# Memory's product ahead of x's tiles: reordering the first block of a two-layer kernel

## The chip, the cores and the metric

The kernel runs on one core of a Trainium2 chip. The metric is the device time of one execution in microseconds (us). Three runs of the kernel before gave 2940.59, 2943.91 and 2949.29; the median is 2943.91.

## The reference

Two residual layers on `x` of 1024 positions by 1024 channels, in float32. The first layer mixes an RWKV-7 branch and a short convolution, adds a cross attention over 256 memory vectors and an MLP; the second layer has a gated delta rule and a stick-breaking attention. The change touches only how the first things that the first layer needs come about. Cut to these:

```
h = rms_norm(x, norm_mix)              # x: 1024 x 1024
p = h @ w_in                           # its first three column tiles used here: lora inputs
mem_n = rms_norm(mem, norm_mem)        # mem: 256 x 1024
k, v = split(mem_n @ w_kv, 2)          # w_kv: 1024 x 2048
```

and `rms_norm(x, g) = x * rsqrt(mean(x * x) + 1e-6) * g`.

## The kernel before

The program is a row of blocks with a barrier of all engines between them. The first block is built by `start_to_loras`. It has three helpers: `Start` loads and turns `mem` and `x`, `MemoryKeys` makes the product of `mem` with `w_kv`, and `MixNorm` makes the normalised x, `h`.

Every product is made of float32 numbers as three products of rounded numbers (type fp32r): a number is split into a rounded part (`hi`) and a remainder (`lo`), and TensorE adds hi by hi, lo by hi and hi by lo. ScalarE makes the rounded part and VectorE subtracts it from the number for the remainder.

The work of the block, in the order of the kernel before:

- **Loads.** SyncE's queue issues the ten tiles of 128 rows (two of `mem`, eight of `x`, 512 KB each), then the first two rows of weights of `w_kv`, then some of the small vectors (gains and biases), then further rows. There are 16 rows of weights: 0 to 7 for the keys, 8 to 15 for the values, each of 128 by 1024. They go through four raw buffers, and row j from 4 on waits until row j - 4 has been split (`fetch`). ScalarE's queue issues the other 18 loads of small vectors. All vectors lie as rows of one tile, `vec_rows`, which TensorE turns once (`vec`).
- **Turning.** TensorE transposes each of the ten tiles in eight pieces into a pair of PSUM banks (`turn`, L4299), and VectorE copies the pair out (`copy`, L4338). ScalarE sums the squares of each tile (`square`, L4319). After eight tiles TensorE turns the vectors (L4311) and then tiles 8 and 9.
- **Memory.** ScalarE multiplies `mem` by its gain and rounds (`mem_hi`, L4330), and VectorE makes `mem_lo` (L4352). The gain comes from the turned vectors. Only when all eight parts are done and all ten tiles copied does the first product begin.
- **Rows.** Per row of `w_kv`: ScalarE rounds (`kv_hi`, L4394), VectorE subtracts (`kv_lo`, L4398), TensorE does 12 matmuls of 128x512 (`products`, L4408). The pairs hi and lo have three buffers, so ScalarE begins row j when TensorE has finished row j - 3.
- **Between rows.** Behind row 1 TensorE spreads the 1024 factors of x's norm over all partitions (`spread_row`, L4466), from a diagonal that VectorE makes (`factors`, L4457), and ScalarE keeps them (`keep_row`, L4472). For each of eight parts k of x, VectorE scales (`scale`, L4480), ScalarE rounds (`round`, L4485) and VectorE subtracts (`subtract`, L4490). In rows 4 to 15 VectorE does one of these two operations per row, in turn; parts 6 and 7 come behind row 15. Behind row 9 TensorE turns the keys (`turn_keys`, L4425); ScalarE has taken them from the banks (L4417) and copies them back (L4432), and SyncE stores them, behind the fetch of row 12 and ahead of those of rows 13 to 15.
- **w_in.** Three tiles of `w_in` go through `round_tile` on ScalarE and `subtract_tile` on VectorE (L177), and TensorE makes 48 matmuls with each (L280). VectorE mixes their results for the lora stage (L4648, L4650), and GpSimd splits the next block's first two tiles (L161, L164).

GpSimd makes constants and masks in the first 14 us (L2205 and its neighbours).

Of the kernel before, what the change touches and what calls it, by code (L numbers as in the profile page):

```python
# [11 lines left out]
P = 128  # L12
SEQ = 1024
HALF = 512
D = 1024
# [17 lines left out]
    ("r_k", 4), ("ln_x_w", 4), ("ln_x_b", 4), ("conv_w", 12), ("norm_xattn", 8), ("norm_mem", 8),  # L33
# [4151 lines left out]
class Vectors:  # L4185
# [40 lines left out]
    def load(self, eng, group):  # L4226
        eng.wait_ge(self.cleared, 1)
        for dst, src in self.pieces(group):
            eng.dma_start(dst, src).then_inc(self.loaded[group], 16)


class Start:
# [4 lines left out]
    def __init__(self, c):  # L4237
        self.c, d = c, c.dram
        self.tiles = [d["mem"][0, t * P:(t + 1) * P, :] for t in range(2)] + [d["x"][0, t * P:(t + 1) * P, :] for t in range(TILES)]
        self.xin = at(c, 24576, "x_in", [P, len(self.tiles), D])  # L4240
# [8 lines left out]
        self.vec_turned, self.vec_copied = c.sem("vec_turned"), c.sem("vec_copied")  # L4249
        self.mem_rounded, self.mem_split = c.sem("mem_rounded"), c.sem("mem_split")  # L4250
# [4 lines left out]
    def load(self, sp):  # L4255
        for t, src in enumerate(self.tiles):
            sp.dma_start(self.xin[:, t], src).then_inc(self.x_in[t], 16)
# [35 lines left out]

    def turn(self, pe, t):
        c = self.c
        pe.wait_ge(self.x_in[t], 16)
        wait(pe, self.copied, t - 1)
        for k in range(KT):
            last = pe.transpose(c.ps[:, 2 * (t % 2) + k // 4, (k % 4) * P:(k % 4 + 1) * P], self.xin[:, t, k * P:(k + 1) * P],  # L4299
                                c.ident[:])  # L4300
        last.then_inc(self.turned, 1)

    def pe(self, pe):
        c = self.c
        pe.wait_ge(c.begun, 1)
        for t in range(8):
            self.turn(pe, t)
        for g in range(2):
            pe.wait_ge(self.vectors.loaded[g], self.vectors.total[g])
        for s in range(2):  # L4310
            last = pe.transpose(c.ps[:, 4, s * P:(s + 1) * P], self.vectors.rows[:, s, :], c.ident[:])  # L4311
        last.then_inc(self.vec_turned, 1)
        for t in range(8, 10):
            self.turn(pe, t)

    def square(self, act, t):
        act.wait_ge(self.x_in[t], 16)
        wait(act, self.squared, t - 1)
        act.activation(self.junk[t % 2][:], self.xin[:, t], ACT.Square, accum_out=self.sums[:, t:t + 1]).then_inc(self.squared, 1)  # L4319

    def act(self, act):
        c = self.c
        for t in range(8):
            self.square(act, t)
        act.wait_ge(self.vec_turned, 1)
        act.copy(c.vec[:], c.ps[:, 4, 0:2 * P]).then_inc(self.vec_copied, 1)
        act.wait_ge(self.vec_copied, 1)
        act.wait_ge(self.copied, 2)
        for k in range(KT):
            act.activation(self.mem_hi[:, k], self.mem_t[:, k], ACT.Copy, scale=vec(c, "norm_mem", k)).then_inc(self.mem_rounded, 1)  # L4330
        for t in range(8, 10):
            self.square(act, t)

    def copy(self, dve, t):
        c = self.c
        dve.wait_ge(self.turned, t + 1)
        dst = c.x[:, :, (t - 2) * P:(t - 1) * P] if t > 1 else self.mem_t[:, :, t * P:(t + 1) * P]
        dve.tensor_copy(dst, c.ps[:, 2 * (t % 2):2 * (t % 2) + 2, :].rearrange("p b (k n) -> p (b k) n", n=P)).then_inc(self.copied, 1)  # L4338

    def dve(self, dve):  # L4340
        c = self.c
        for t in range(8):
            self.copy(dve, t)

        dve.wait_ge(self.copied, 2)
        for k in range(KT):
            if k == 3:
                self.copy(dve, 8)
            if k == 6:
                self.copy(dve, 9)  # L4350
            dve.wait_ge(self.mem_rounded, k + 1)
            dve.scalar_tensor_tensor(out=self.mem_lo[:, k], in0=self.mem_t[:, k], scalar=vec(c, "norm_mem", k),  # L4352
# [3 lines left out]
class MemoryKeys:  # L4356
# [6 lines left out]
    def __init__(self, c, start):  # L4363
# [5 lines left out]
        self.keys = at_h(c, 32768 + 20480, "mem_keys", [P, KT, N_MEM])  # L4369
# [2072 lines left out]
```

## Time and profile before

| what | us |
|---|---|
| median of three runs (2940.59 to 2949.29) | 2943.91 |
| the profiled execution | 2940.22 |
| its span, first to last instruction | 2938.5 |
| TensorE busy in the span (96%) | 2808.3 |
| VectorE busy | 1604.6 |
| ScalarE busy | 1120.5 |
| GpSimd busy | 1325.8 |
| the first block, from the start to the next block's first matmul | 114.75 |

The profile is of one execution. Busy times are summed over the instructions of an engine. A row of the timeline gives the start, the time from the first instruction's start to the last one's end of a group that belongs together, the engine (PE is TensorE, PEld its weight loads, DVE VectorE, ACT ScalarE, POOL GpSimd, SPq SyncE's queue), line and operation, and in brackets how long the engine was idle before and what ended it. The granted clock is that of TensorE as a share of 2.4 GHz.

### The profile page before, as it was taken

How to read it: one execution, taken by the hardware profiler on the slowest of the kernel's cores; microseconds unless marked ns; L12 is line 12 of the kernel's file. 1: busy time of each engine (PE TensorE's matmuls, PEld its weight loads, DVE VectorE, ACT ScalarE, POOL GpSimd, SP SyncE). 2: the span in 40 equal slices, each digit the busy share in tenths (PEclk: the TensorE clock that was granted, in tenths of full speed). 3: DMA queues.
4: the chain of work that ended last, by engine and by line, in shares of the span. 5: the costliest groups of instructions: out<-in, count | busy, mean ns of one | idle time of the engine just before them, and what ended most of it. 6: DMA issues, size and time to landing. Idle time of an engine off the chain costs nothing. (4 is left out here: it accounts for less than half of the span.)

```text
span 2938.5 us, 48523 instructions
## 1 busy us (share of the span) xinstructions
PE 2808.3 (96%) x19890; PEld 2247.0 (76%) x19890; DVE 1604.6 (55%) x1907; ACT 1120.5 (38%) x1781; POOL 1325.8 (45%) x987
## 2 busy tenths in 40 slices
PE   7999788999999999999999999999999899999999
PEld 6777677778878876788888888677787678866677
DVE  5555444863465434555555554767768435357661
ACT  5433223554311123424444444333323335567310
POOL 1331213677645430347777775211211457745552
PEclk9999999999999999999999999999999999999999
DMA  5342433343171111122322233131234524421243
GB/s 206 108 158 95 129 89 95 109 139 90 36 229 43 50 51 44 43 79 88 99 88 92 88 97 104 36 94 52 86 99 139 164 85 123 127 83 62 68 139 127
DMA packets 318509, 288.93 MB, mean 98 GB/s; under 512 B 47858, under 2 KB 270249, under 8 KB 315610
## 3 DMA queue, kind: packets, MB, share of 16 engines
q1 hardware_dynamic: 318042, 285.89, 31.8%
q8 instruction: 153, 2.51, 0.4%
q14 instruction: 58, 0.48, 0.1%
q10 hardware_dynamic: 256, 0.07, 0.0%
HBM read 214.86 MB, written 70.65 MB: 97 GB/s over the span
## 5 line engine op out<-in xcount | busy, mean ns | idle before, releaser
L855 POOL TENSOR_TENSOR op_lo<-w_raw,op_hi 128x512 fp32r<-128x512 f32 x172 | 222.1, 1299 | 238.3 <-ACT op_hi L844 237.7
L280 PE MATMUL ps<-h_hi,w_hi 128*128 128x512 f32 x960 | 310.3, 404 | 5.3 <-POOL w_lo L177 3.7
L280 PE MATMUL ps<-h_lo,w_hi 128*128 128x512 f32 x960 | 297.9, 392 | 0.0
L280 PE MATMUL ps<-h_hi,w_lo 128*128 128x512 f32 x960 | 297.5, 391 | 0.0
L161 POOL TENSOR_TENSOR w_hi<-w_raw,ones 128x1024 fp32r<-128x1024 f32 x54 | 132.0, 2444 | 300.9 <-PE ps L280 161.2
L280 PEld LDWEIGHTS ps<-h_hi,w_hi 128*128 128x128 f32 x960 | 179.2, 189 | 62.2 <-issue 22.9
L280 PEld LDWEIGHTS ps<-h_hi,w_lo 128*128 128x128 f32 x960 | 181.2, 189 | 38.9
L280 PEld LDWEIGHTS ps<-h_lo,w_hi 128*128 128x128 f32 x960 | 181.0, 189 | 38.7
L177 POOL TENSOR_TENSOR w_lo<-w_raw,w_hi 128x1024 fp32r<-128x1024 f32 x30 | 73.1, 2437 | 303.8 <-ACT w_hi L172 303.8
L164 POOL TENSOR_TENSOR w_lo<-w_raw,w_hi 128x1024 fp32r<-128x1024 f32 x54 | 145.4, 2693 | 4.2
L1784 DVE TENSOR_TENSOR x_t<-x_t,ps 128x512 f32<-128x512 f32 x144 | 96.2, 685 | 83.7 <-PE ps L910 56.8
L844 ACT CAST op_hi<-w_raw 128x512 fp32r<-128x512 f32 x167 | 102.5, 620 | 84.6 <-POOL w_raw L860 27.6
L280 PE MATMUL ps<-branch_hi,w_hi 128*128 128x512 f32 x384 | 120.2, 394 | 7.0 <-POOL w_lo L164 5.5
L5370 DVE RECIPROCAL p_root<-p_root 128x1024 f32<-128x1024 f32 x16 | 104.8, 6547 | 36.3 <-ACT p_root L5224 36.1
L860 POOL TENSOR_TENSOR w_raw<-w_raw 128x512 f32<-128x512 f32 x92 | 122.3, 1329 | 3.6
L280 PE MATMUL ps<-branch_lo,w_hi 128*128 128x512 f32 x384 | 118.7, 391 | 0.0
L280 PE MATMUL ps<-branch_hi,w_lo 128*128 128x512 f32 x384 | 118.7, 390 | 0.0
L6198 POOL TENSOR_TENSOR sb_weight<-sb_weight,sb_left 128x512 f32<-128x512 f32 (+3 forms) x96 | 84.9, 896 | 71.2 <-DVE sb_left L6352 70.6
L6352 DVE TENSOR_TENSOR_SCAN sb_left<-ps,sb_left,ones 128x512 f32<-128x512 f32 (+3 forms) x96 | 92.4, 1004 | 34.2 <-ACT ps L6298 32.8
L897 PE MATMUL ps<-h_hi,op_hi 128*128 128x512 f32 x256 | 99.8, 390 | 0.0
L897 PE MATMUL ps<-h_hi,op_lo 128*128 128x512 f32 x256 | 99.6, 389 | 0.0
L897 PE MATMUL ps<-h_lo,op_hi 128*128 128x512 f32 x256 | 99.6, 389 | 0.0
(736 smaller groups left out, 7321.1 us busy)
## 6 DMA issues: line engine op xcount, KB each, us to landing
w_raw<-in_w_in_dram SPq DMA_DIRECT2D x91, 512.0 KB, 4.8
mix_gates<-mix_sig SPq DMA_DIRECT2D x64, 256.0 KB, 2.3
w_raw<-in_w_up_dram SPq DMA_DIRECT2D x32, 512.0 KB, 4.2
w_raw<-in_w_down_dram SPq DMA_DIRECT2D x32, 512.0 KB, 3.5
kv_raw<-in_w_kv_dram SPq DMA_DIRECT2D x16, 512.0 KB, 6.0
mix_gate_b<-mix_gates SPq DMA_DIRECT2D x32, 256.0 KB, 4.6
mlp_t3h<-mlp_kept_t SPq DMA_DIRECT2D x6, 1024.0 KB, 5.0
mlp_t3l<-mlp_kept_t SPq DMA_DIRECT2D x6, 1024.0 KB, 4.9
```

The lines of the kernel that those rows point to most:

```text
L161: pool.tensor_tensor(c.w_hi[:, s], c.w_raw[:, s], c.ones[:].unsqueeze(1).broadcast_to([P, KT, P]), ALU.mult).then_inc(c.w_rounded, 1)
L164: pool.tensor_tensor(c.w_lo[:, s], c.w_raw[:, s], c.w_hi[:, s].bitcast(F32), ALU.subtract).then_inc(c.w_split, 1)
L177: eng.tensor_tensor(c.w_lo[:, s], c.w_raw[:, s], c.w_hi[:, s].bitcast(F32), ALU.subtract).then_inc(c.w_split, 1)
L280: last = pe.matmul(o, w[:, s, k], a[:, k - offset, (half + h) * width:(half + h + 1) * width], start=(k == kts[0] and w is c.w_hi and a is ...
L844: act.copy(self.hi(o)[:], src).then_inc(self.rounded, 1)
L855: pool.tensor_tensor(self.lo(o)[:], src, self.hi(o)[:].bitcast(F32), ALU.subtract).then_inc(self.pooled, 1)
L860: pool.tensor_tensor(out, a, b, op).then_inc(self.pooled, 1)
L897: last = pe.matmul(out, w[:, k], a(k), start=start and k == 0 and w is w_hi and a is hi, stop=stop and k == HK - 1 and w is w_lo, skip_gro ...
L1784: dve.tensor_tensor(part, part, ps[:, down_banks[g, d][bank][side]], ALU.add).then_inc(down_free, 1)
L5370: v.mark(dve.reciprocal(root[:], root[:]))
L6198: pool.tensor_tensor(weight[:, n % 4, hd, 0:width], weight[:, n % 4, hd, 0:width], left[:, n % 2, hd, 1:width + 1], ALU.mult).then_inc(wei ...
L6352: dve.tensor_tensor_scan(l[:, hd, 0:width][:, ::-1], ps[:, 2 * (n % 2) + hd, 0:width][:, ::-1], c.ones[:, 0:1].broadcast_to([P, width]), l ...
```

## The change

The vector `norm_mem` gets a load and a transpose of its own, so `mem` no longer waits for all vectors. SyncE issues the two tiles of `mem`, then rows 0 and 1 of `w_kv`, and then x's tiles with rows 2 and 3 among them. Six of the first group's vector loads move from ScalarE's queue to SyncE's, and SyncE's vector loads stand behind row 4. TensorE turns only `mem` ahead of row 0; x's tiles are turned behind rows 0 to 5, and the vectors and the spreading stand behind row 6. Each row of the keys waits only for its own part of `mem`. ScalarE's and VectorE's queues are put in a matching order, so that the sums of squares stand between the roundings of rows 3 to 7. The scaling of x begins at row 8 and takes a part per row: at rows 9 to 15 VectorE does kv_lo, one scaling and one remainder. The remainders of the three `w_in` tiles go to GpSimd. The keys, the x tiles and the gain have other places in memory, and the store of the keys now stands ahead of row 15 only. The core of the diff:

```
-        self.xin = at(c, 24576, "x_in", [P, len(self.tiles), D])
+        self.xin = [at_h(c, 12288 + 4096 * t, f"x_in{t}", [P, D]) if t < 4 else
+                    c.nc.alloc_sbuf_tensor_at(f"x_in{t}", [P, D], F32, offset=c.w_base + 4096 * (t - 4)) for t in range(len(self.tiles))]
...
+    def banks(self, t):
+        return 2 * t if t < 2 else 4 + 2 * (t % 2)
+
     def turn(self, pe, t):
+        c, bank = self.c, self.banks(t)
+        pe.wait_ge(self.x_in[t], 16)
+        if t == 3:
+            pe.wait_ge(self.gain_copied, 1)
+        if t > 3:
+            pe.wait_ge(self.copied, t - 1)
...
+    def turn_gain(self, pe):
         c = self.c
+        pe.wait_ge(self.gain_loaded, 16)
+        pe.transpose(c.ps[:, 6, 0:KT], self.gain_rows[:], c.ident[0:KT, 0:KT]).then_inc(self.gain_turned, 1)
+
+    def turn_vectors(self, pe):
...
+        pe.wait_ge(self.copied, 10)
...
+    def take_gain(self, act):
+        act.wait_ge(self.gain_turned, 1)
+        act.copy(self.gain[:], self.c.ps[:, 6, 0:KT]).then_inc(self.gain_copied, 1)
+        act.wait_ge(self.gain_copied, 1)
+        act.wait_ge(self.copied, 2)
...
     def fetch(self, sp, j):
-        if j < 2:
-            pass
-        elif j < self.RAW:
-            sp.wait_ge(self.start.turned, 2)
-            sp.wait_ge(self.start.squared, 2)
-        else:
+        if j >= self.RAW:
             sp.wait_ge(self.split, j - self.RAW + 1)
...
     def products(self, pe, j):
         pe.wait_ge(self.split, j + 1)
+        if half == 0:
+            pe.wait_ge(self.start.mem_split, k + 1)
...
             @block.sync
-                start.load(sp)
-                for j in range(2):
-                    memory.fetch(sp, j)
+                start.load(sp, 0, 1)
+                memory.fetch(sp, 0)
+                memory.fetch(sp, 1)
+                start.load(sp, 2, 3)
+                memory.fetch(sp, 2)
+                start.load(sp, 4, 5)
+                memory.fetch(sp, 3)
+                start.load(sp, 6, 7, 8, 9)
+                memory.fetch(sp, 4)
                 start.vectors.load(sp, 1)
-                for j in range(2, 4):
-                    memory.fetch(sp, j)
+                start.vectors.load(sp, 0, 12)
+                memory.fetch(sp, 5)
                 start.store_masks(sp)
-                for j in range(4, 13):
+                for j in range(6, 15):
                     memory.fetch(sp, j)
                 sp.wait_ge(memory.keys_copied, 4)
                 sp.dma_start(c.scratch["mem_k"] ...
-                for j in range(13, 16):
-                    memory.fetch(sp, j)
+                memory.fetch(sp, 15)
...
             @block.gpsimd
                 start.pool(pool)
+                weights.subtract_tile(pool, 0, 0)
+                pool.wait_ge(memory.keys_stored, 16)
+                for u in range(1, 3):
+                    weights.subtract_tile(pool, 0, u)
...
             @block.tensor
-                start.pe(pe)
-                pe.wait_ge(start.mem_split, KT)
-                pe.wait_ge(start.copied, 10)
+                pe.wait_ge(c.begun, 1)
+                start.turn(pe, 0)
+                start.turn(pe, 1)
+                start.turn_gain(pe)
                 for j in range(16):
                     memory.products(pe, j)
-                    if j == 1:
+                    for t in ((2,), (3,), (4,), (5, 6), (7,), (8, 9))[j] if j < 6 else ():
+                        start.turn(pe, t)
+                    if j == 6:
+                        start.turn_vectors(pe)
                         norm.spread_row(pe)
...
             @block.scalar
-                start.vectors.load(act, 0)
-                start.act(act)
+                start.load_gain(act)
+                start.vectors.load(act, 0, 0, 12)
                 memory.round(act, 0)
+                start.take_gain(act)
+                start.round(act, 0, 1)
                 memory.round(act, 1)
+                start.round(act, 2, 3, 4, 5, 6, 7)
+                memory.round(act, 2)
+                for j in range(3, 8):
+                    for t in range(2 * (j - 3), 2 * (j - 2)):
+                        start.square(act, t)
+                    memory.round(act, j)
                 norm.root(act)
+                memory.round(act, 8)
+                start.take_vectors(act)
                 norm.keep_row(act)
-                for j in range(4, 16):
+                for j in range(9, 16):
                     memory.round(act, j)
-                    if j == 10:
+                    if j == 9:
...
-                    if j % 2:
-                        norm.round(act, (j - 5) // 2)
+                    norm.round(act, j - 9)
...
             @block.vector
-                start.dve(dve)
+                start.copy(dve, 0)
+                start.copy(dve, 1)
                 memory.subtract(dve, 0)
+                start.subtract(dve, 0, 1)
                 memory.subtract(dve, 1)
+                start.subtract(dve, 2, 3, 4, 5, 6, 7)
+                start.copy(dve, 2)
+                memory.subtract(dve, 2)
+                start.copy(dve, 3)
+                for j in range(3, 8):
+                    memory.subtract(dve, j)
+                    for t in ((4,), (5, 6), (7,), (8, 9), ())[j - 3]:
+                        start.copy(dve, t)
                 norm.factors(dve)
-                memory.subtract(dve, 2)
-                memory.subtract(dve, 3)
-                for j in range(4, 16):
+                for j in range(8, 16):
                     memory.subtract(dve, j)
-                    if j % 2 == 0:
-                        norm.scale(dve, (j - 4) // 2)
-                    else:
-                        norm.subtract(dve, (j - 5) // 2)
-                    if j == 13:
-                        dve.wait_ge(memory.keys_stored, 16)
-                weights.subtract_tile(dve, 0, 0)
-                for k in range(6, 8):
-                    norm.scale(dve, k)
-                    norm.subtract(dve, k)
-                for u in range(1, 3):
-                    weights.subtract_tile(dve, 0, u)
+                    norm.scale(dve, j - 8)
+                    if j > 8:
+                        norm.subtract(dve, j - 9)
+                norm.subtract(dve, 7)
```

## Rows read from the trace of the kernel before

**Rows 1.** The page's costliest groups; the last number before the bar is the mean ns.

```profile
L177 POOL TENSOR_TENSOR w_lo<-w_raw,w_hi 128x1024 fp32r<-128x1024 f32 x30 | 73.1, 2437 | 303.8 <-ACT w_hi L172 303.8
```

**Rows 2.** Busy time by windows of the first block; start:end, length, engines, clock, DMA, GB/s.

```profile
29.70:34.50 4.80, 4.78 (x12) 3.87 (x13) 3.60 (x4) 2.10 (x3) 0.00 (x0) 0.56 0.68 211
34.50:81.60 47.10, 44.69 (x201) 36.17 (x200) 31.95 (x27) 25.66 (x30) 0.00 (x0) 1.00 0.53 168
81.60:114.70 33.10, 32.83 (x145) 26.84 (x143) 18.34 (x9) 14.02 (x15) 11.42 (x5) 1.00 0.33 98
10.00:20.00 10.00, 5.27 (x41) 4.20 (x39) 7.08 (x6) 7.96 (x16) 3.80 (x16) 1.00 1.03 397
```

**Rows 3.** Timeline of TensorE up to its first product.

```profile
4.71 6.30 PE L4299 MATMUL ps<-ident,x_in 128*128 128x128 f32 x32 [4.71 <-DMA x_in<-in_mem_dram]
11.47 2.20 PE L4299 MATMUL ps<-ident,x_in 128*128 128x128 f32 x16 [0.47 <-DVE x_t L4338]
...
20.90 0.66 PE L4311 MATMUL ps<-ident,vec_rows 128*128 128x128 f32 x2 [4.75 <-DMA vec_rows<-in_sb_k_gain_dram]
...
29.72 1.19 PE L4408 MATMUL ps<-kv_hi,mem_hi 128*128 128x512 f32 x2 [5.29 <-DVE kv_lo L4398]
```

**Rows 4.** Timeline of TensorE from its first product to the next block.

```profile
37.28 1.88 PE L4466 MATMUL ps<-mix_diag,ones 128*128 128x512 f32 x4
38.60 1.03 PE L4408 MATMUL ps<-kv_hi,mem_hi 128*128 128x512 f32 x2
...
60.82 1.91 PE L4425 MATMUL ps<-ident,w_raw 128*128 128x128 f32 x16
62.48 0.71 PE L4408 MATMUL ps<-kv_hi,mem_hi 128*128 128x512 f32 x2
...
73.31 0.73 PE L4408 MATMUL ps<-kv_hi,mem_hi 128*128 128x512 f32 x2 [2.41 <-DVE kv_lo L4398]
...
81.62 0.62 PE L280 MATMUL ps<-h_hi,w_hi 128*128 128x512 f32 x2
...
114.75 0.70 PE L280 MATMUL ps<-h_hi,w_hi 128*128 128x512 f32 x2 [0.32 <-PEq L4521]
```

**Rows 5.** Timeline of VectorE, ScalarE and SyncE's queue, 8 to 98 us.

```profile
8.40 1.22 DVE L4338 COPY mem_t<-ps 128x1024 f32<-128x1024 f32 x1 [0.48 <-PE ps L4299]
...
27.27 0.87 DVE L4352 SCALAR_TENSOR_TENSOR mem_lo<-mem_t,vec,mem_hi 128x256 fp32r<-128x256 f32 x2
...
31.17 1.23 DVE L4457 TENSOR_TENSOR mix_diag<-ident,square_sums 128x1024 f32<-128x1024 f32 x1
...
39.20 1.01 ACT L4472 COPY mix_row<-ps 128x1024 f32<-128x1024 f32 x1 [3.37 <-PE ps L4466]
...
56.58 2.42 ACT L4417 ACTIVATE w_raw<-ps,square_sums 128x512 f32<-128x512 f32 x4
...
64.51 3.03 SPq L4388 DMA_DIRECT2D kv_raw<-in_w_kv_dram  x3
...
74.31 1.22 DVE L4398 TENSOR_TENSOR kv_lo<-kv_raw,kv_hi 128x1024 fp32r<-128x1024 f32 x1
75.44 1.28 DVE L4480 SCALAR_TENSOR_TENSOR mix_whole<-x_t,vec,mix_row 128x1024 f32<-128x1024 f32 x1
76.64 1.22 DVE L4398 TENSOR_TENSOR kv_lo<-kv_raw,kv_hi 128x1024 fp32r<-128x1024 f32 x1
...
97.12 3.30 DVE L4650 SCALAR_TENSOR_TENSOR lora_mixed<-lora_mixed,vec,lora_plain 128x1024 f32<-128x1024 f32 x1
```

**Rows 6.** Timeline of GpSimd: two steps of the masks, and a remainder.

```profile
10.78 0.58 POOL L2205 TENSOR_SCALAR_AFFINE_SELECT level_temp<-level_temp 128x64 f32<-128x64 f32 x2
...
96.09 3.25 POOL L164 TENSOR_TENSOR w_lo<-w_raw,w_hi 128x1024 fp32r<-128x1024 f32 x1
```

**Rows 7.** Loads issued at 0.8 and at 64.5 us; the last number is us to landing.

```profile
x_in<-in_mem_dram SPq DMA_DIRECT2D x1, 512.0 KB, 3.8
...
kv_raw<-in_w_kv_dram SPq DMA_DIRECT2D x1, 512.0 KB, 6.4
```

More of the change, by code:

```diff
@@ L4224, in pieces, with load @@
                     done += m
-    def load(self, eng, group):
+    def load(self, eng, group, first=0, last=None):
         eng.wait_ge(self.cleared, 1)
-        for dst, src in self.pieces(group):
+        for dst, src in list(self.pieces(group))[first:last]:
             eng.dma_start(dst, src).then_inc(self.loaded[group], 16)
@@ L4253, in __init__, with load, load_gain @@
         scratch(c, "masks", [P, N_MASKS, BLOCK])
[L4255 to L4257 removed]
+    def load(self, sp, *which):
+        for t in which:
+            sp.dma_start(self.xin[t][:], self.tiles[t]).then_inc(self.x_in[t], 16)
+    def load_gain(self, act):
+        act.dma_start(self.gain_rows[:], self.c.dram["norm_mem"].rearrange("a (n p) -> (a n) p", p=P)).then_inc(self.gain_loaded, 16)
     def store_masks(self, sp):
@@ L4318, in square @@
         wait(act, self.squared, t - 1)
[L4319 to L4324, printed above, removed]
-        act.wait_ge(self.vec_turned, 1)
[L4326 to L4332, printed above, removed]
+        act.activation(self.junk[t % 2][:], self.xin[t][:], ACT.Square, accum_out=self.sums[:, t:t + 1]).then_inc(self.squared, 1)
@@ new lines, in take_gain, with take_vectors, round @@
+    def take_gain(self, act):
[3 more added lines that the diff above has]
+        act.wait_ge(self.copied, 2)
+    def take_vectors(self, act):
+        act.wait_ge(self.vec_turned, 1)
+        act.copy(self.c.vec[:], self.c.ps[:, 6, 0:2 * P]).then_inc(self.vec_copied, 1)
+    def round(self, act, *which):
+        for k in which:
+            act.activation(self.mem_hi[:, k], self.mem_t[:, k], ACT.Copy, scale=self.gain[:, k:k + 1]).then_inc(self.mem_rounded, 1)
@@ L4334, in copy @@
     def copy(self, dve, t):
-        c = self.c
+        c, bank = self.c, self.banks(t)
         dve.wait_ge(self.turned, t + 1)
         dst = c.x[:, :, (t - 2) * P:(t - 1) * P] if t > 1 else self.mem_t[:, :, t * P:(t + 1) * P]
[L4338 to L4350, printed above, removed]
+        dve.tensor_copy(dst, c.ps[:, bank:bank + 2, :].rearrange("p b (k n) -> p (b k) n", n=P)).then_inc(self.copied, 1)
@@ L4351, in dve, with subtract @@
+    def subtract(self, dve, *which):
+        for k in which:
             dve.wait_ge(self.mem_rounded, k + 1)
-            dve.scalar_tensor_tensor(out=self.mem_lo[:, k], in0=self.mem_t[:, k], scalar=vec(c, "norm_mem", k),
+            dve.scalar_tensor_tensor(out=self.mem_lo[:, k], in0=self.mem_t[:, k], scalar=self.gain[:, k:k + 1],
                                      in1=self.mem_hi[:, k].bitcast(F32), op0=ALU.mult, op1=ALU.subtract).then_inc(self.mem_split, 1)
```

46 lines of the change are left out of this document (20 added, 26 removed).

## The prediction

> **What bounds the kernel now.** The windows come first [rows 2], behind one line of the page that the second part needs [rows 1]. The kernel is one span of 2938.5 us in which TensorE is nearly always busy, and the change touches only its first 114.75 us, the block that `start_to_loras` builds. A barrier ends that block: the next block's first matmul starts at 114.75, 0.32 us after TensorE's last one here [rows 4]. VectorE and ScalarE are busy for 18.3 and 14.0 us of the last 33.1 [rows 2]. So the block ends when TensorE ends, and a microsecond taken out of TensorE's queue comes off the whole time, because later blocks are not touched and their first loads are issued by events that move with it.
>
> The timeline of TensorE's own instructions shows where it isn't working [rows 3, 4]. Up to its first product with the memory at 29.72 it waits 4.71 us for the first tile, 0.47 and once more less for VectorE to empty banks, 4.75 for the small vector loads that landed behind twelve big ones, and 5.29 for VectorE, which rounds all of `mem` before the first weights. From 29.72 on it stands still once, 2.41 us before row 13. The 51.90 us from 29.72 to 81.62 are: row 0 in 4.80 us (12 matmuls at a granted clock of 0.56, so mostly at 1.2 GHz) [rows 2]; spreading the mix factors 1.32 (37.28 to 38.60); turning the keys 1.66 (60.82 to 62.48); the stall of 2.41; what is left, 41.7, is 15 rows of 2.78. After 81.62 come 33.1 us of w_in products with no gap.
>
> **The change, part by part.** TensorE's work is the same but for one tiny transpose; what moves is the order. The eight x tiles are turned between rows 0 to 5 instead of ahead of row 0. The sum is when the chain of products ends, counted forward.
>
> *First product.* The memory tiles are still loads one and two. The first tile landed 3.8 us after its issue, and 512 KB at the 397 GB/s of a full queue is 1.3 us [rows 2, 7]. Counting tiles in the new order, w row 0 lands at about 7.3 and row 1 at 8.6; all of x is in by 22, row 4 by 23.3, and behind it twelve small vector loads. In the trace before seven of those and the two last big tiles lay between x and the vectors' 20.90, which leaves about 0.2 us each, so row 5 lands near 27. TensorE reaches rows 4 and 5 only after 27 and 31. The transfers are cover, not bound. VectorE's second copy of `mem` still runs 8.40 to 9.62 [rows 5]. Behind it come kv_lo 0 (1.22) and the first mem_lo (0.45, two took 0.87), so the first product could start at 11.3. ScalarE is in time: it issues 12 vector loads instead of 18 and is ready at about 7.3.
>
> There is one thing on that path that the rows only show elsewhere. At 97.12 an operation of VectorE with two SBUF inputs took 3.30 us where its like takes 1.28, and GpSimd's at 96.09 took 3.25 against a mean of 2.44 [rows 1, 5, 6]. VectorE's ended 1.1 us after GpSimd's, as if each had the memory to itself. In the early block GpSimd is making masks until about 14.4, in steps of about 0.3 us [rows 6], and VectorE's subtractions now fall into that time (before, only copies from PSUM did). Each of the two on the path can wait 0 to 0.35 us. Taken: 0.3 together, 11.6; bounds 11.3 and 12.1. The later six mem_lo and kv_lo 1 slip by at most the 4 us of masks that are left, to 18; row 2 needs its weights at 21.4. The Trainium skill's page "SBUF — State Buffer", section "SBUF: two separate sides", says that the pair of ports is an exclusive lock, taken by a VectorE operation with two SBUF inputs against a GpSimd one that reads SBUF. By it the selects count and the memsets don't, and the start would be 11.6; if it didn't hold for selects, 11.3. No row of the trace before has a subtraction against a select.
>
> *Rows 0 to 6.* Row 0 costs 4.80 again: TensorE's first 32 transposes took 6.30 us where later ones take 1.10 for eight [rows 3], so it starts slow, and it stops at 8.3, before that had lifted, and waits over 3 us. If the clock were up, row 0 would cost 2.78. From 11.6: row 0 to 16.4, six rows of 2.78 to 33.1, eight tiles of 1.10 to 41.9. VectorE keeps up in it: of its 1.22 us per copy and per kv_lo, two in a 3.9 us turn, never more than three.
>
> *The factors.* Tiles 8 and 9 are turned before row 6, that is by 39.1. VectorE then has copy 8, copy 9 and kv_lo 7 in its queue (38.1 to 41.7), then the reciprocal 0.22 and the diagonal 1.23, to 43.2. TensorE turns the vectors (0.45) to 42.3 and waits 1.0 for it: 43.3. Spreading costs 1.32, row 7 ends at 47.4. Before, this wait did not exist; its cost is what is late behind the last copies.
>
> *Rows 8 to 15.* Here is the place to look. Before, VectorE did three operations for every two TensorE rows. Now rows 9 to 15 each bring three: kv_lo, a scaling, a remainder. From one start to the next these take 1.13 to 1.14, 1.20 and 1.14 [rows 5], 3.48 us a row against TensorE's 2.78. VectorE's lead: the row copy (1.01 us, begun 1.9 after the spreading starts) [rows 5] ends at 46.2, and scaling 0 starts there. Kv_lo 9 and scaling 1 follow to 49.8. Remainder 0 waits for ScalarE, which must first take row 8's four banks (2.42 us from 47.5) [rows 5] and round 0, to 50.9. From there a row every 3.48: kv_lo 10, 11, 12, 13, 14, 15 are ready at 53.3, 56.8, 60.2, 63.7, 67.2, 70.7. TensorE would be ready for them at 54.5 (after turning the keys), 57.3, 60.1, 63.0 and so on: it waits 0.1 for row 12 and 0.7 each for rows 13, 14, 15. Total 2.2.
>
> *The old stall.* Row 13 waited 2.41 us because its load stood on SyncE's queue behind the store of the keys: issued at 64.5, it landed at 70.9 [rows 5, 7]. Now only row 15 and the w_in tiles are behind that store, which is issued near 58.7; row 15 lands by 65 and w_in 0 at 67 to 70.5 against a need at 69.4. So 2.41 goes away.
>
> *w_in's first tile.* Its remainder goes to GpSimd, 2.44 us a tile instead of 1.22 [rows 1]. Rounded at about 70.4, it is ready at 73.1, or at 74.3 if one operation of VectorE goes first. TensorE is there at 73.5. Taken 0.3, bounds 0 and 1. Tiles 1 and 2 have 10 us each to spare, and the next block's tiles, queued on GpSimd behind them, are split long before their use.
>
> Sum: 11.6 + 4.8 + 41.7 (15 rows) + 8.8 + 0.45 + 1.0 + 1.32 + 1.66 + 2.2 + 0.3 = 73.8, against 81.62. The gain is 7.8 us. In other words: the first product comes 18.1 us sooner and a stall of 2.4 goes, 9.25 us of transposes fall into the chain instead, and 3.5 us of new waits are made. The profiled execution's own 2940.22 becomes 2932.4; it lies 3.7 us under the median of the runs, so of 2943.91 it leaves 2936.1.
>
> **The rivals.** 0.3%, here 8.8 us, is about what a measurement of this kernel tells from no change, and the forecast lies just inside it.
>
> (a) *The clock is up sooner.* Row 0 then costs 2.78, and 2.0 more is gained: 9.8, 2934.1. For it: only 3.3 us lie between the last transpose and the first product. Against: a pause of 4.75 us before was followed by slow transposes and one of 5.3 by a slow row [rows 2, 3], and the engine has not been fast yet. With the chance that some wait (factors, row 12 on) is smaller than reckoned: 0.36 for over 8.8 us. The Trainium skill's "TensorE: Matmul & The Clock Gate", section "What's actually happening", has the slow clock as the default that activity lifts; by that, the row stays slow.
>
> (b) *VectorE paces more than I count.* Handshakes with ScalarE of 0.3 us on each of the 21 operations of rows 9 to 15 would make a row 4.4 us: 6 us gone of which TensorE's slack takes none, and the gain is about 2, 2942. Before, such handshakes showed as short idle times of VectorE, but when it had time to spare. Chance 0.13.
>
> (c) *The change does not do what it says:* weights land behind x and TensorE stands. A start at 20 instead of 11.6 would eat it, at 2943 or so. Full-queue speed speaks against it; w row 0 would have to land 8 us late. Chance 0.03.
>
> (d) *Slower.* Mixing transposes and fp32r products with waits in between could keep TensorE at 1.2 GHz through rows 1 to 6 and all x tiles. Each row then costs 2.0 more and eight tiles 0.8 each: 18 us, net 10 slower, 2954. It decides from the point where more than four rows stay slow (8 us: nothing gained). Against: TensorE has no wait between 11.6 and 42.3, and in the trace before the clock rose 4 us into such a stretch. With all else that could go so: 0.04.
>
> **How the numbers follow.** The forecast, 5 to 8.8 us gained, has 0.44; (a) 0.36; (b) 0.13; (c) 0.03; (d) 0.04. Likeliest time 2936, its own range 2933.5 to 2940 with the uncertainty of the start (0.8), of the clock (2), of the tile (1) and of the waits. The range for 8 in 10 takes in (a) and (b): 2930.5 to 2942.5. Faster by over 0.3%: 0.37; within: 0.58 (forecast, b, c and the smaller half of measuring spread); slower: 0.05.
>
> **What the profile would show.** First product at 11.3 to 12.1 with kv_lo 0 or mem_lo as its releaser. Row 0 in 4.8 us, the clock at 1.0 from about 16. A wait of 1.0 ahead of the spreading, released by the diagonal. No stall at row 13 by a load, but short waits on kv_lo in rows 12 to 15. First w_in matmul at 73.8, next block at 106.9. Wrong would be: rows 1 to 6 at 5 us (d), VectorE idle between its operations after 47 (b), a wait of TensorE released by a load (c), subtractions of 2 us and more before 15 us (the shared memory port, larger than taken).

## The result, and the profile after

The changed kernel takes 2928.36 us (median of 5 runs, 2924.89 to 2929.46) against 2943.91 (2940.59 to 2949.29, 5 runs): a ratio of 0.9946, interval 0.9935 to 0.9956, 15.6 us less. The forecast was 2936.1 with a range down to 2930.5, so the time lies 2.1 us below the range, on the side of "faster" that had 0.37. The profiled execution takes 2927.02, its span 2925.3; TensorE is busy 2803.3 us of it.

The first block of the changed kernel, TensorE's timeline. It answers to [rows 3, 4]; x and a number at a line's end tell how many instructions are drawn together.

```profile
4.63 3.65 PE L4312 MATMUL ps<-ident,x_in 128*128 128x128 f32 x16 [4.63 <-DMA x_in<-in_mem_dram]
8.21 0.27 PE L4318 MATMUL ps<-ident,mem_gain_rows 8*128 8x8 f32 x1
11.22 1.19 PE L4410 MATMUL ps<-kv_hi,mem_hi 128*128 128x512 f32 x2 [2.73 <-DVE mem_lo L4357]
...
16.41 1.04 PE L4312 MATMUL ps<-ident,x_in 128*128 128x128 f32 x8
17.21 0.70 PE L4410 MATMUL ps<-kv_hi,mem_hi 128*128 128x512 f32 x2
...
27.30 1.91 PE L4312 MATMUL ps<-ident,x_in 128*128 128x128 f32 x16
28.96 0.71 PE L4410 MATMUL ps<-kv_hi,mem_hi 128*128 128x512 f32 x2
...
39.92 0.38 PE L4326 MATMUL ps<-ident,vec_rows 128*128 128x128 f32 x2
41.48 1.95 PE L4472 MATMUL ps<-mix_diag,ones 128*128 128x512 f32 x4 [1.18 <-issue]
42.87 1.02 PE L4410 MATMUL ps<-kv_hi,mem_hi 128*128 128x512 f32 x2
...
59.03 0.73 PE L4410 MATMUL ps<-kv_hi,mem_hi 128*128 128x512 f32 x2 [0.17 <-DVE kv_lo L4398]
...
62.50 0.73 PE L4410 MATMUL ps<-kv_hi,mem_hi 128*128 128x512 f32 x2 [0.45 <-DVE kv_lo L4398]
...
72.29 0.62 PE L280 MATMUL ps<-h_hi,w_hi 128*128 128x512 f32 x2
```

The first product starts at 11.22 instead of 29.72, released by VectorE's `mem_lo`. From there TensorE has one wait of 1.18 ahead of the spreading and four short ones on `kv_lo`, and it comes to w_in at 72.29, 9.3 us sooner than in [rows 4]. The waits of TensorE up to 110 us (total, times, longest) say that nothing else is left:

```profile
PE ps L4312 <- DMA x_in<-in_mem_dram: 4.6, 1, 4.6
PE ps L4410 <- DVE mem_lo L4357: 2.7, 1, 2.7
PE ps L4410 <- DVE kv_lo L4398: 1.5, 4, 0.4
PE ps L4472 <- issue: 1.2, 1, 1.2
PE ps L280 <- PEq L4528: 0.3, 1, 0.3
```

The next block starts at 105.41. So 9.3 us come from the first block by these two profiles, and 15.6 by the medians. The rest of the text is about the difference.

### The profile page after: what moved, and what is told of

It is laid out like the page before. It is cut to its first block and busy times, and to the rows that moved or that the text cites. A ratio compares the mean times of both kernels' runs of the same rounds, so it can differ in the third digit from the quotient of the medians.

```text
span 2925.3 us, 48530 instructions
## 1 busy us (share of the span) xinstructions
PE 2803.3 (96%) x19891; PEld 2241.3 (77%) x19891; DVE 1595.4 (55%) x1904; ACT 1119.1 (38%) x1782; POOL 1335.0 (46%) x990
## 5 line engine op out<-in xcount | busy, mean ns | idle before, releaser
L177 POOL TENSOR_TENSOR w_lo<-w_raw,w_hi 128x1024 fp32r<-128x1024 f32 x33 | 80.3, 2434 | 361.7 <-ACT w_hi L172 361.7
L164 POOL TENSOR_TENSOR w_lo<-w_raw,w_hi 128x1024 fp32r<-128x1024 f32 x54 | 144.3, 2672 | 4.2
```

The source lines that it names most:

```text
L164: pool.tensor_tensor(c.w_lo[:, s], c.w_raw[:, s], c.w_hi[:, s].bitcast(F32), ALU.subtract).then_inc(c.w_split, 1)
```

## The experiments

**The spread of both kernels, and the block's end moved.** The first question was whether the 15.6 us are real and whether they hang on when the later blocks start. Four kernels: both kernels again, and both with ScalarE copies behind the block's work, so that the block ends later. In the changed one:

```
                weights.done(act, 0, 2)
                for n in range(14):
                    c.a_steps.wait(act)
                    c.a_steps.mark(act.copy(c.ps[:, 7, 0:512], c.x[:, 0, 0:512]))
```

(in the kernel before 2 copies of 320.)

> The changed kernel once more, unaltered. In its first profile the next block began 9.4 us sooner than before, but the span was 13.2 us shorter and the median of the runs 15.5 us. Theory L (luck): the 4 to 6 us beyond the first block come from TensorE's slow-clock stretches, which fall differently on the later blocks in each execution; then this ratio is nearer 0.9968 (9.4 us) and this profile's later part differs from the first one's by some microseconds. Theory S (systematic): the later blocks are really shorter in the changed kernel, and the ratio is 0.9946 again. First block either way: next block's first matmul at 105.4, within 0.2.

> The changed kernel with 14 copies of 128x512 one after another on ScalarE at the end of its first block, behind TensorE's last product there (they compute nothing that is used): some 9.4 us of pause, so that the later blocks start when they do in the kernel before. Theory L: time equals that of the kernel before, ratio 1.000, later part of the profile 2820 to 2824 us like any other. Theory S by start time (the later blocks' slow-clock stretches depend on when they start): ratio 1.000 too, but e4 then gains about 5 us. Theory S by code (something in the changed program makes later blocks shorter wherever they start): ratio 0.998, 6 us under before.

> The kernel before, unaltered, for a second profile and five more runs. Both theories: ratio 1.000. What it is to show is the spread of the part behind the first block: theory L expects that part (2823.7 us in the first profile) to differ by 2 to 4 us here, with the slow-clock stretches in other places; theory S expects 2823 to 2829 again and the same places.

> The kernel before with two copies of 128x320 on ScalarE at the end of its first block: about 1 us of pause. [...] Theories L and S by code: ratio 1.000 to 1.0005, 1 us slower.

Measured: the changed kernel 2927.25 (2922.8 to 2936.39, 6 runs; ratio 0.996, 0.9945 to 0.9976); the padded one 2935.83 (12 runs, 0.999, 0.998 to 1.0); the kernel before 2941.92 (11 runs) and with its pad 2943.95 (12 runs), against 2939.89 in 29 runs on that chip. The pad of about 8.6 us (next block at 114.03) costs 8.6 us by the medians, 8.8 by the means, no more. So the gain is real, some 12 to 16 us by the pairs of medians, and in this pair the time follows the block's end one for one (the last kernel below does not bear that out). The small pad costs 2.0, against some 1 us of it: not to be told apart. A third set of runs of the changed kernel was taken later:

> The changed kernel once more beside e10, to set its ratio firmer and for a third profile. Theory L (9.4 to 11.5 us in the first block, where the kernel before has one or two more slow-clock stretches; later blocks the same on average): ratio 0.9961 to 0.9968. Theory S: 0.9946.

It took 2924.14 (2920.84 to 2930.08, 5 runs), ratio 0.9948 (0.9934 to 0.9962). Over the three chips on which the changed kernel ran, 54 runs of the kernel before have a mean of 2941.3 (standard deviation 3.4) and 16 of the changed one 2927.5 (4.0): 13.8 with a standard error of 1.1.

The second profile of the kernel before has the same start as the first and a longer stall. It spreads the factors at 37.02 (37.28 in [rows 4]), and row 13 begins at 73.05 behind a pause of 2.39, but then four pairs in it run at half clock, 0.85 us apart, which the first profile does not have behind its 2.41:

```profile
37.02 1.88 PE L4466 MATMUL ps<-mix_diag,ones 128*128 128x512 f32 x4
...
73.05 0.73 PE L4408 MATMUL ps<-kv_hi,mem_hi 128*128 128x512 f32 x2 [2.39 <-DVE kv_lo L4398]
...
74.54 1.03 PE L4408 MATMUL ps<-kv_hi,mem_hi 128*128 128x512 f32 x2
75.38 1.05 PE L4408 MATMUL ps<-kv_hi,mem_lo 128*128 128x512 f32 x2
...
77.94 0.64 PE L4408 MATMUL ps<-kv_hi,mem_lo 128*128 128x512 f32 x2
...
116.09 0.70 PE L280 MATMUL ps<-h_hi,w_hi 128*128 128x512 f32 x2 [0.32 <-PEq L4521]
```

Four unpadded profiles of the kernel before (two of them of shortened kernels, below) have the next block at 114.75, 116.09, 116.05 and 116.58, mean 115.9; five of the changed kernel at 105.41, 104.62, 105.58, 104.35 and 104.66, mean 104.9. The block is 11.0 us shorter on average, not 9.3. Of the 1.1 that the kernel before needs beyond its first profile, 0.4 arise before the spreading (37.02 to 38.43, mean 37.7) and 0.7 at the old stall: the slow pairs above in one, a pause of 3.03 and 3.07 instead of 2.41 in the two others. The changed kernel's other 0.5 is row 0, which took 4.34 to 4.42 in three of its five profiles instead of 5.19.

**Where the rest is: kernels that end early.** The later blocks are left out: `build` ends behind the first block (cut1) or behind the scan (cut2) and writes `c.x` out.

```
-        late = first_block(c)
-        renew(c)
-        second_block(c, out, late)
+        cut_block(c)
+        write_out(c, out)
```

> The kernel before, ended behind its first block: all later blocks are left out, and x is written out as it lies. Its time is for the difference to e13. Theory L (all that is systematic is in the first block): the difference of the medians is 13 to 14 us. Rival (the first block gives what the profiles show and the rest lies further on or is chance): 9.3 to 11.5.

> The changed kernel, ended behind its first block in the same way. Theory L: 13 to 14 us under e12. Rival: 9.3 to 11.5 us under it. About 125 us in all.

> The kernel before, ended behind the scan (three blocks: start, features, scan; the rest is left out). About 520 us. For the difference to e15: if the scan's slow-clock stretches favour the changed kernel's start time, 13 to 15 us; if the scan only adds chance, the same difference as e12 and e13, with a spread of 2 to 4 us from run to run.

> The changed kernel, ended behind the scan in the same way. 9 to 12 us under e14 if the scan adds chance alone, 13 to 15 if it favours the earlier start.

Cut behind the first block: 129.81 (129.51 to 131.32) against 119.40 (118.66 to 120.39), 10.4 us (11.0 by the means). Behind the scan: 520.07 (517.51 to 524.56) against 504.68 (504.49 to 507.39), 15.4 us. About 5 us are thus gained in features and scan, by a change that does not touch them. One candidate was the moment at which they start. So the changed kernel was started late: 16 copies of ScalarE go ahead of its first load, SyncE waits for them, the first tile is turned at 15.78, the next block begins at 117.33.

```
+                act.wait_ge(filled, 1)
+                for n in range(16):
+                    wait(act, late, n)
+                    act.copy(c.ps[:, 7], c.x[:, 0, 0:HALF]).then_inc(late, 1)
...
+                sp.wait_ge(late, 16)
```

> e15's kernel (the changed one, ended behind the scan) with 16 copies of 128x512 one after another on ScalarE ahead of its first load, for which all loads wait: everything starts 10 to 11 us later, about where the scan of the kernel before starts. If the scan's length follows from when it starts: 520 us, like e14. If it follows from the program: 504.7 + 10.5 = 515, with a spread under 2 us. If it is chance: 515 to 520 with a spread of 2 to 3.

> e14 again (the kernel before, ended behind the scan). Chance: a median anywhere from 516 to 522. Otherwise 520 again.

> e15 again (the changed kernel, ended behind the scan). Chance: a median anywhere from 504.5 to 510, and a difference to e17 nearer 10.4 than 15.4. Otherwise 504.7 again, and 15 us under e17.

The late one took 516.92 (515.82 to 519.29); the two others, again, 522.96 (517.99 to 524.76) and 505.2 (503.29 to 509.89). All runs of the pair cut behind the scan together, 10 and 10, have means of 521.4 and 505.6: 15.8 us, 4.8 more than the 11.0 behind the first block, with a standard error of 1.1. The next block of the late kernel starts 12.4 us after the 104.9 of the others, and 505.6 + 12.4 = 518.0: it is late by its delay and keeps the short scan, although its scan begins later than in the kernel before (next block at 117.33 against 115.9). At this one later moment, at least, the start is not the cause.

The profiles say in part what differs in the scan, and not why. The features take 185.4 us in every profile but that of the padded changed kernel, where they take 2.2 more. The scan took 204.6, 199.9, 207.4, 200.9 and 204.3 in profiles of the kernel before (the third is the padded one) and 201.3, 207.7, 200.7, 199.8, 198.3, 200.4 (padded) and, in the late one, 200.6 of the changed kernel. In each there are stretches at half clock, near the scan's start and at other places from one execution to the next. The longest scans are of both kinds, and seven profiles against five don't separate them; the cut runs do, by 4.8 us.

It is not the clock that separates them. Both kernels cut behind the scan, from the scan's first matmul to its last and in one step of it (before, then changed; the figures behind the length are the five engines, TensorE first, and the clock behind them):

```profile
301.72:500.26 198.54, 161.03 (x5665) 141.90 (x5665) 84.25 (x192) 57.89 (x120) 49.07 (x57) 0.97 0.35 91
419.82:433.33 13.51, 10.78 (x394) 9.80 (x398) 4.99 (x11) 3.85 (x8) 2.85 (x4) 1.00 0.43 115
```

```profile
290.02:487.46 197.44, 162.59 (x5665) 143.62 (x5665) 84.33 (x192) 57.89 (x120) 48.80 (x57) 0.96 0.35 92
410.13:421.34 11.21, 10.51 (x394) 9.66 (x398) 4.86 (x11) 3.85 (x8) 2.84 (x4) 1.00 0.51 139
```

TensorE's busy time is not less in the changed kernel (162.5 to 167.7 us in its seven profiles, 161.0 to 165.1 in the five of before); it stands idle less, 33.2 to 37.6 us, mean 34.9, against 36.0 to 40.0, mean 37.7. One place differs beyond chance, the step from the eighth to the ninth copy of `scan_y`: 13.4 to 14.5 us in all five, 11.0 to 12.3 in all seven. The step ahead of it is shorter in the kernel before (10.6 to 11.0 against 11.0 to 12.1), so the two together give 1.5 us. The waits of TensorE in the step (before, then changed):

```profile
PE ps L2573 <- issue: 1.3, 1, 1.3
PE ps L2618 <- issue: 1.0, 1, 1.0
PE ps L2573 <- DVE scan_ab L2821: 0.5, 1, 0.5
```

```profile
PE ps L2573 <- issue: 0.4, 1, 0.4
PE ps L2573 <- DVE scan_ab L2821: 0.3, 1, 0.3
```

"Issue" is a wait for nothing that the profile shows: 2.2 to 2.7 us in the step before, 0.2 to 1.4 after. What it is stays open.

**The order alone.** All x tiles turned and copied ahead of row 0; gain, loads and everything else as in the change.

```
                 start.turn_gain(pe)
+                for t in range(2, 10):
+                    start.turn(pe, t)
                 for j in range(16):
                     memory.products(pe, j)
-                    for t in ((2,), (3,), (4,), (5, 6), (7,), (8, 9))[j] if j < 6 else ():
-                        start.turn(pe, t)
```

(VectorE: the copies 2 to 9 go ahead of `memory.subtract(dve, 2)`.) This kernel and the next three ran once each. Single runs of one kernel have a standard deviation of 3 to 5 us, so the argument goes by the start of the next block in the profile, which moves by 1.2 us in the changed kernel.

> The changed kernel with one part undone: x's eight tiles are turned and copied ahead of row 0 again (the early gain, the order of the loads and all the rest stay). Theory A (the gain is the time in which the tiles' turning and landing lie beside rows): the last tile lands at 22, the first product comes at about 23 to 24 instead of 11.2, and the rows lose eight tiles of 0.8 each, so w_in begins 5 to 6 us later than 72.3, at about 78, and the next block at 111. A second stretch of slow clock would add 2. Rival: the rows are held by VectorE and ScalarE anyway and most of the gain stays: next block at 106 to 107.

One run, 2935.49 (before on that chip 2941.93); the next block starts at 108.12, 2.7 later than with the change. TensorE:

```profile
11.75 3.68 PE L4312 MATMUL ps<-ident,x_in 128*128 128x128 f32 x16 [3.73 <-DMA x_in<-in_x_dram]
16.08 6.13 PE L4312 MATMUL ps<-ident,x_in 128*128 128x128 f32 x32 [0.65 <-DVE x_t L4352]
22.71 2.19 PE L4312 MATMUL ps<-ident,x_in 128*128 128x128 f32 x16 [0.51 <-DVE x_t L4352]
24.66 0.71 PE L4410 MATMUL ps<-kv_hi,mem_hi 128*128 128x512 f32 x2
```

It waits 3.73 for the first x tile, and the tiles are slow until some 21 us. But row 0 then runs at full clock from its first pair, which gives 2.4 back. That is why the order costs half of what was expected. Of the 11 us, the other 8 belong to what this kernel keeps: the gain of its own, which frees `mem`, the order of the loads, and the place of the store, which takes away the old stall (2.4 us and more). Only the store is undone by itself, below; gain and loads were not taken apart.

**VectorE's pace.** The remainders of h move to GpSimd, ahead of its w_in tile.

```
                 start.pool(pool)
+                for k in range(7):
+                    norm.subtract(pool, k)
                 weights.subtract_tile(pool, 0, 0)
+                norm.subtract(pool, 7)
...
                     norm.scale(dve, j - 8)
-                    if j > 8:
-                        norm.subtract(dve, j - 9)
-                norm.subtract(dve, 7)
```

> The changed kernel with the eight remainders of h (h_lo) on GpSimd instead of VectorE, so that VectorE has two operations a row. Theory A (the two engines take turns at the memory when both have two SBUF inputs): a row needs 1.13 + 1.20 + 2.4 = 4.7 us, GpSimd's 2.4 hold up kv_lo, TensorE waits about 2 us at each of rows 11 to 15, next block 6 to 10 us later than 105.4. Rival (they run side by side): the four waits on kv_lo (together 2.3 us lost in rows 12 to 15) go, next block 1 to 2 us sooner.

One run, 2943.05; the next block starts at 115.94, 10.5 later than with the change. Its waits, then VectorE and GpSimd in two of its rows:

```profile
PE ps L4410 <- DVE kv_lo L4398: 7.3, 5, 1.5
...
PE ps L280 <- issue: 2.8, 1, 2.8
```

```profile
61.93 3.42 DVE L4487 SCALAR_TENSOR_TENSOR mix_whole<-x_t,vec,mix_row 128x1024 f32<-128x1024 f32 x1
65.27 1.21 DVE L4398 TENSOR_TENSOR kv_lo<-kv_raw,kv_hi 128x1024 fp32r<-128x1024 f32 x1
66.40 1.27 DVE L4487 SCALAR_TENSOR_TENSOR mix_whole<-x_t,vec,mix_row 128x1024 f32<-128x1024 f32 x1
67.60 3.43 DVE L4398 TENSOR_TENSOR kv_lo<-kv_raw,kv_hi 128x1024 fp32r<-128x1024 f32 x1
```

```profile
61.33 2.93 POOL L4497 TENSOR_TENSOR h_lo<-mix_whole,h_hi 128x1024 fp32r<-128x1024 f32 x1 [0.41 <-ACT h_hi L4492]
66.50 6.78 POOL L4497 TENSOR_TENSOR h_lo<-mix_whole,h_hi 128x1024 fp32r<-128x1024 f32 x2 [2.24 <-ACT h_hi L4492]
```

A third of VectorE's work is gone in these rows and a row takes it longer: 1.2 us become 3.4 where an operation falls behind one of GpSimd's on large SBUF operands, and rows come every 4.5 us. Help from GpSimd costs VectorE about what GpSimd takes. Behind the last wait, 2.8, w_in's first three pairs ran at half clock.

**The old stall.** Rows 13 and 14 are fetched behind the store of the keys again, as before the change.

```
-                for j in range(6, 15):
+                for j in range(6, 13):
                     memory.fetch(sp, j)
                 sp.wait_ge(memory.keys_copied, 4)
...
-                memory.fetch(sp, 15)
+                for j in range(13, 16):
+                    memory.fetch(sp, j)
```

> The changed kernel with the store of the keys ahead of the loads of rows 13 and 14 again, as in the kernel before. Store at 57.3, row 13 then issued at 57.7 and landing 6.4 us later at 64.1; ScalarE needs 1.05 and VectorE 1.2, so row 13 is ready at 66.3 or later where TensorE now begins it at 62.5: 3 to 4 us lost there, of which the shorter waits at rows 14 and 15 give back at most 1.2. Next block at 107.5 to 109. If the store's place does not matter: 105.4.

One run, 2933.66; the next block starts at 110.67, 5.3 later. TensorE and ScalarE around row 13:

```profile
66.92 1.22 PE L4410 MATMUL ps<-kv_hi,mem_hi 128*128 128x512 f32 x2 [4.40 <-DVE kv_lo L4398]
67.93 1.05 PE L4410 MATMUL ps<-kv_hi,mem_lo 128*128 128x512 f32 x2
```

```profile
64.56 1.04 ACT L4394 CAST kv_hi<-kv_raw 128x1024 fp32r<-128x1024 f32 x1 [5.92 <-DMA kv_raw<-in_w_kv_dram]
```

The row that names VectorE as releaser is a late load: ScalarE waited 5.92 for it. And the pause has a second price: the pairs of row 13 start 0.85 us apart instead of 0.455, 2.4 us for the row. The pause and the slow row make 7.0 us (4.6 from the end of row 12 to row 13, and 2.4), less some 2.2 for the three waits on VectorE, which has caught up meanwhile, and the slower first pairs behind them: 4.8. The other 0.5 of the 5.3 is the start of this execution (row 12 begins at 59.51 instead of 59.03). The store's place is thus worth more than the 2.41 of [rows 4].

**Row 0's clock.** 13 more transposes of the identity into an idle bank follow the gain.

```
                 start.turn_gain(pe)
+                for n in range(13):
+                    pe.transpose(c.ps[:, 7, 0:P], c.ident[:], c.ident[:])
```

> The changed kernel with 13 transposes of the identity into a free bank behind the turning of the gain; their results are not used. They fill TensorE's wait from 8.5 to 11.2. Theory A (row 0 is slow because TensorE paused before its clock had risen): row 0 takes 2.7 to 3.5 us instead of 5.2, next block 1.7 to 2.4 sooner than 105.4. Rival (the rise comes by its own time whatever is done): row 0 takes 5.2 again, or the fillers delay it.

One run, 2923.93; the next block starts at 103.72, 1.7 sooner.

```profile
7.94 1.64 PE L4584 MATMUL ps<-ident 128*128 128x128 f32 x13
11.83 0.70 PE L4410 MATMUL ps<-kv_hi,mem_hi 128*128 128x512 f32 x2 [2.25 <-DVE mem_lo L4357]
...
14.64 1.04 PE L4312 MATMUL ps<-ident,x_in 128*128 128x128 f32 x8
```

Row 0 takes 2.81 us instead of 5.19, in spite of the same kind of wait ahead of it; the first product came 0.6 later. In this execution the clock was up when the 13 began (1.64 us for all); in the last kernel below they ran at half clock (2.72 us for 13), and row 0 took 2.84 all the same.

**VectorE's work moved behind row 15, and both.** In rows 10 to 15 VectorE does one operation beside each `kv_lo` instead of two, and the rest of h's work follows row 15; ScalarE's roundings follow that order. In the list s is a scaling, l a remainder of h, w the remainder of w_in's tile 0, which comes back from GpSimd. The last kernel has the transposes as well.

```
+                for j, ops in ((8, "s0"), (9, "s1 l0"), (10, "s2"), (11, "l1"), (12, "s3"), (13, "l2"), (14, "s4"),
+                               (15, "l3 s5 l4 w s6 l5 s7 l6 l7")):
                     memory.subtract(dve, j)
...
```

> The changed kernel with VectorE's queue thinned in rows 10 to 15: beside kv_lo one operation of h per row (two at row 9), as the kernel before had it, and the rest behind row 15, where w_in's products take part k of h only every 1.36 us; the remainder of the first w_in tile is VectorE's again, and ScalarE's order follows. Theory A (rows 12 to 15 go at VectorE's 3.47 us a row): the four waits go, 0.3 + 3 x 0.75 = 2.6 us, w_in begins at about 69.8 instead of 72.3 and the next block at 102.8 to 103.5; part 3 to 7 of h are there in time (h_lo 7 by 77 against a need at 79). Rival (the end is set by the load of row 15 or of w_in's first tile, which land at 64.3 and 66.2): a new wait of 1 to 2 us at row 15 or at w_in, next block at 104 to 105.

> e9 and e8 together: thinned queue of VectorE and the 13 filling transposes. If the two gains add: next block at 102.8 - 1.6 = 101.2 to 101.8, ratio to the kernel before about 0.9950 against 0.9963 of the changed kernel, with later blocks that differ by up to 4 us either way from one profile to the next. If the load of row 15 or w_in's first tile is next in line, the earlier start is lost: 103.

The first took 2924.45 (2922.6 to 2930.74, 4 runs; ratio 0.995, 0.9934 to 0.9966): the waits on `kv_lo` are gone, w_in begins at 69.69 and the next block at 102.94. Both together took 2928.29 (2923.89 to 2931.24, 5 runs; 0.9961, 0.9947 to 0.9974), with the next block at 101.13. By the profile the first block is 4.3 us shorter than with the change, but neither median can be told from the changed kernel's 2924.14 to 2928.36; the scan of that profile took 205.8. By the means the last kernel's 2928.4 lies 0.9 above the changed kernel's 2927.5, where its block, 3.8 us shorter than the mean 104.9, would put it 3.8 below; the standard error of the difference is 1.7. So what is saved in the first block did not all come off the whole time here, and where it went is open.

## Why the prediction was wrong

The order of the argument held; two sizes in it did not, and both lay on the same side.

**The step that failed: "later blocks are not touched".** The working took the gain of the first block as the whole gain. Cut behind the first block the kernels differ by 10.4 us (11.0 by the means), cut behind the scan by 15.4 and 17.8 (15.8 by the pooled means). So about 5 us lie behind the first block, and since the features take the same, in the scan. The start's moment as the cause does not fit the late kernel (516.9, not 521). What is left is something that the changed program brings along. In the profiles it shows as idle time of TensorE in the scan, 2.8 us less on average, 1.5 of it at one place, and not in the clock. Which part of the change does it was not found, and the cause stays open. It does not hold for every program with the changed block: the six variants of it (from the order alone to the last kernel) have scans of 200.5 to 205.8 us, mean 203.2, like the 203.4 of before, with TensorE idle for 36.8 on average, between the two. That it is partly chance of the runs is not excluded: whole kernels differ by 13.8 ± 1.1, which leaves 2.8 beside the block's 11.0.

**The first block's gain, 7.8, was too small.** Against the same profile of before it is 9.3, against the mean of several 11.0. Term by term:

- First product 11.6: 11.22. Row 0 4.80: 5.19, at half clock as taken. The early rivals (a) and (d) are decided: the clock did not come up for good before row 0's end in any profile of the changed kernel (in the second one row 0 began fast, fell back behind two pairs and took 4.34), and from row 1 on it stayed up. More than 8.8 us were gained all the same, the outcome to which (a) gave 0.36: that it came true is luck, for neither a fast row 0 nor smaller waits gave the most of it.
- Eight tiles 8.8: 6.5. This is the mis-sized term. The 1.10 a tile came from [rows 3], where each group of eight transposes also holds a pause for VectorE's copy and the last one's run-out. Behind a row TensorE takes 0.80 (16.41 to 17.21) and 0.83 (two in 1.66). 2.3 us.
- 15 rows 41.7: 42.7. The first pair behind each change of work takes 0.53 to 0.57 instead of 0.455, and 0.86 behind the spreading; small, of the other sign.
- Vectors and the wait for the factors 1.45: 1.56. Spreading 1.32: 1.39. Keys 1.66: 1.66.
- Waits in rows 12 to 15, 0.1 + 3 x 0.7 = 2.2: by the starts of the rows 0.3 + 3 x 0.6 = 2.1, of which the profile calls 0.17 and 3 x 0.45 idle. VectorE's turn is 3.47 us, against 3.48. Rival (b) is wrong.
- Old stall gone: yes, and undoing that alone costs 4.8. The 2.41 taken for it is the least of four profiles: 3.1 on average, with the slow pairs counted.
- w_in's tile 0.3: 0. Rival (c) is wrong: no load holds TensorE behind the first tile.
- Sum 73.8: 72.29. The rest of the way to 11.0 is mostly in the base: the one profile of before on which the sum was made ended its block soonest of four (114.75 against 116.05 to 116.58), 0.4 of the 1.1 by its start and 0.7 by its stall.

**The shared SBUF port.** The prediction gave 0.3 us for subtractions beside the masks. The rows, VectorE and then GpSimd:

```profile
9.46 1.21 DVE L4398 TENSOR_TENSOR kv_lo<-kv_raw,kv_hi 128x1024 fp32r<-128x1024 f32 x1
10.59 0.87 DVE L4357 SCALAR_TENSOR_TENSOR mem_lo<-mem_t,mem_gain,mem_hi 128x256 fp32r<-128x256 f32 x2
...
69.29 3.42 DVE L4487 SCALAR_TENSOR_TENSOR mix_whole<-x_t,vec,mix_row 128x1024 f32<-128x1024 f32 x1
```

```profile
9.84 1.37 POOL L2205 TENSOR_SCALAR_AFFINE_SELECT level_temp<-level_temp 128x64 f32<-128x64 f32 x2
...
69.23 2.40 POOL L177 TENSOR_TENSOR w_lo<-w_raw,w_hi 128x1024 fp32r<-128x1024 f32 x1 [52.42 <-ACT w_hi L172]
```

VectorE keeps its 1.21 and 0.87; it is GpSimd's pair of selects that takes 1.37, where the pair at the same place in the kernel before, at 9.85, took 0.65 (the pairs at 7.5 and 8.8, with no such subtraction beside them, take 0.97 and 0.77 in both kernels). At 69.2 GpSimd's large subtraction starts 0.06 us ahead of VectorE's scaling, keeps its 2.40, and VectorE takes 3.42. Of these two the earlier keeps its time and the later one waits; with longer queues on both sides, as in the run with h's remainders on GpSimd, both are drawn out (GpSimd's to 2.93 and 3.4, VectorE's to 3.42). The Trainium skill's "SBUF — State Buffer", section "SBUF: two separate sides", calls the shared pair an exclusive lock between the two engines; the trace agrees that they take turns, and shows what the prediction had the wrong way round: here it was GpSimd's short operations that waited for VectorE's long ones. In the queue here the 3.42 fell behind the last `kv_lo` and cost TensorE nothing.

## What to carry to other kernels

Take the duration of a moved piece of work from a place where it has the neighbours that it will have: the tiles' 1.10 held waits that stayed behind, and that was 2.3 of 7.8 us. Where a forecast of 0.3% is wanted, one profile of the kernel before is too few, since its first block's end moves by 1.8 us between four profiles, and "the rest is not touched" is itself a term with a spread: cut the kernel behind the changed part and behind the next one to size it. And before giving VectorE's work to GpSimd, look whether both will work on SBUF at once, for then they take turns.

## What was not expected of the hardware

- The kernel's executions differ by some 0.2% to 0.3% (2940.59 to 2949.29) with the same instructions, and profiles show stretches at the clock's lower level (1.2 GHz) in other places and lengths each time: the kernel before's scan took 199.9 to 207.4 us.
- A pause of 4.40 us of TensorE at full clock (2.4 GHz) was followed by a whole row at half of it (pairs 0.85 us apart); a pause of 1.18 us (ahead of the spreading) and one of 2.25 us (behind the 13 more transposes) were not. In between it goes either way: of the kernel before's stall at row 13, pauses of 2.39 and 2.42 us had four to five slow pairs behind them, and pauses of 2.41, 3.03 and 3.07 had none.
- The granted clock that the profile gives for a window can mislead: for 11.2 to 16.4 us of the changed kernel the windows view gives 1.00 while row 0's pairs are 0.85 us apart. The distance of matmuls decides.
